# Two projection steps in token halves, with their weights loaded ahead of the third x tile, in a fused hybrid attention layer

## The reference

```
def rmsnorm(x, g):
    y = xf * lax.rsqrt(jnp.mean(xf * xf, axis=-1, keepdims=True) + RMS_EPS)
    return (y * g.astype(jnp.float32)).astype(x.dtype)
...
    h = rmsnorm(x, norm_g)
    proj = jnp.einsum('bsd,dc->bsc', h, w_in)
    a_qkv, z_a, b_qkv, z_b, r_a, r_b = jnp.split(proj, offs, axis=-1)
    # three dilated groups and MoBA on slices of proj, gated by silu(z)
    merged = sigmoid(r_a + b_merge[:D]) * y_a + sigmoid(r_b + b_merge[D:]) * y_b
    return x + jnp.einsum('bsd,de->bse', merged, w_out)   # then a last rmsnorm
```

## Time and profile before

| | us |
|---|---|
| median of 3 runs | 429.53 (429.46 to 429.69) |
| the profiled execution, its own time | 429.92 |
| its span, first to last instruction | 428.1 |
| PE busy | 417.7, 98% of the span |
| DVE, ACT, POOL busy | 302.8, 232.0, 220.9 |

### The profile page before, as it was taken

The page is one execution under the profiler, slowest core; times in us unless marked ns, Lnnn a source line. Parts: engine busy times, 40 slices in busy tenths (PEclk is TensorE's granted clock), DMA queues, the critical chain, the costliest instruction groups (busy, mean ns, idle before and its releaser), DMA issues.

```text
span 428.1 us, 7122 instructions
## 1 busy us (share of the span) xinstructions
PE 417.7 (98%) x2526; PEld 372.5 (87%) x2526; DVE 302.8 (71%) x520; ACT 232.0 (54%) x487; POOL 220.9 (52%) x158
## 2 busy tenths in 40 slices
PE   7899999999999999999999999999999999999994
PEld 6789998889889988998888888889999999988884
DVE  3879946385856777657865773696686768589956
ACT  5745557554864764657656563454454545532634
POOL 5954533252655634574459655444335433734790
PEclk9999999999999999999999999999999999999998
DMA  8893454937899768222421335540443134199905
GB/s 272 250 262 102 152 163 143 280 132 260 278 303 388 290 213 273 100 100 54 144 99 50 100 127 205 196 136 14 122 138 108 48 116 136 38 410 393 418 7 198
DMA packets 49187, 77.23 MB, mean 180 GB/s; under 512 B 4440, under 2 KB 39296, under 8 KB 47616
## 3 DMA queue, kind: packets, MB, share of 16 engines
q1 hardware_dynamic: 44256, 67.91, 47.9%
q10 hardware_dynamic: 4896, 8.86, 5.7%
HBM read 55.73 MB, written 14.74 MB: 165 GB/s over the span
## 4 chain that ended last, share of the span: by engine, by line
PE 94%; DMA 2%; ACT 1%; DVE 1%; issue 1%; SPq 0%; DVEq 0%; ACTq 0%
PE ps L1183 15%; PE ps L1187 15%; PE ps L1184 15%; PE ps L1408 5%; PE ps L1407 5%; PE ps L1406 5%; PE ps L1224 4%; PE ps L1226 4%; PE ps L1225 4%; PE ps L1296 4%; PE ps L1277 3%; PE ps L1455 3%; PE ps L1453 3%; PE ps L1454 3%; PE ps L1315 2%; PE ps L1337 2%
## 5 line engine op out<-in xcount | busy, mean ns | idle before, releaser
L993 POOL TENSOR_TENSOR w_lo<-raw,w_hi 128x1024 fp32r<-128x1024 f32 x39 | 96.8, 2483 | 103.5 <-ACT w_hi L1507 103.5
L1183 PE MATMUL ps<-hT_hi,w_hi 128*128 128x512 f32 x240 | 95.7, 399 | 1.1 <-DVE hT_lo L1913 1.1
L1187 PE MATMUL ps<-hT_lo,w_hi 128*128 128x512 f32 x240 | 93.8, 391 | 0.0
L1184 PE MATMUL ps<-hT_hi,w_lo 128*128 128x512 f32 x240 | 93.6, 390 | 0.0
L1075 POOL TENSOR_TENSOR w_lo<-raw,w_hi 128x512 fp32r<-128x512 f32 (+1 forms) x34 | 42.5, 1270 | 49.5 <-ACT w_hi L1529 49.5
L1187 PEld LDWEIGHTS ps<-hT_lo,w_hi 128*128 128x128 f32 x240 | 45.0, 188 | 9.9
L1183 PEld LDWEIGHTS ps<-hT_hi,w_hi 128*128 128x128 f32 x240 | 45.1, 188 | 8.4 <-issue 1.3
L1184 PEld LDWEIGHTS ps<-hT_hi,w_lo 128*128 128x128 f32 x240 | 45.2, 188 | 7.0
L1224 PE MATMUL ps<-w_hi,hT_hi 128*128 128x256 f32 x160 | 45.2, 283 | 0.0
L1226 PE MATMUL ps<-w_lo,hT_hi 128*128 128x256 f32 x160 | 44.7, 279 | 0.0
L1225 PE MATMUL ps<-w_hi,hT_lo 128*128 128x256 f32 x160 | 44.6, 279 | 0.0
(11 more groups left out here) (279 smaller groups left out, 1048.0 us busy)
## 6 DMA issues: line engine op xcount, KB each, us to landing
raw<-in_w_in SPq DMA_DIRECT2D x25, 1024.0 KB, 5.6
KTs<-KTs SPq DMA_DIRECT2D x20, 256.0 KB, 4.4
folds<-folded_early SPq DMA_DIRECT2D x4, 1024.0 KB, 9.3
wq_raw<-in_w_out SPq DMA_DIRECT2D x4, 1024.0 KB, 9.7
folded<-folds SPq DMA_DIRECT2D x4, 1024.0 KB, 6.4
t_three<-output_weight_sums SPq DMA_DIRECT2D x2, 2048.0 KB, 11.5
output_weight_sums<-ws_parts ACTq DMA_DIRECT2D x6, 512.0 KB, 6.1
raw<-in_w_out SPq DMA_DIRECT2D x3, 1024.0 KB, 5.0
```

The source lines that it names most:

```text
L993: nc.gpsimd.tensor_tensor(ring(w_lo, n, kt), src, ring(w_hi, n, kt).bitcast(F32), ALU.subtract).then_inc(lo_ready, 1)
L1183: pe.matmul(out, wh, hh, start=(k == 0), stop=False)
L1184: pe.matmul(out, wl, hh, start=False, stop=False)
L1187: return pe.matmul(out, wh, hl, start=False, stop=(k == kts - 1))
```

## The change

SP now issues x 0 and x 1, then the weights of steps 0 and 1 in two transfers of 512 KB, split by k (4 groups of 128 features each, 256 columns wide) and not by column, and then x 2 and x 3. Steps 0 and 1 are run together and in two halves of 256 tokens. The first half needs x 0 and x 1 only. PE turns these two, ACT and DVE split them by themselves (256 tokens a piece, 8 pieces), and PE runs the 48 products of 256 columns of the first half, both steps interleaved by k. Ahead of the last k it turns x 2 and x 3; then it finishes the first half and runs the 48 products of the second. The turned tiles no longer fit one bank each, because banks 0 and 1 hold the running results: a pair of tiles has six banks, two of them used twice, which adds waits of ACT and PE on hT_lo.

POOL splits the weights of steps 0 and 1 in four pieces of two k, each with both steps in it, high and low. The squares of x 1, x 2 and x 3 are now summed by ACT for the low half of the features and by DVE for the high half; DVE scales the low half and ACT the high half, except that DVE scales both halves of x 1. All these lie between the pieces of the first half on ACT and DVE.

```
-            for i in range(TT):
+            for i in range(2):
+                load_rows(i)
+            for e in range(2):
+                ks = slice(4 * e, 4 * e + 4)
+                sp.dma_start(first[:, ks, :], w_in_t[:, ks, at:at + 256]).then_inc(first_half_in[e], 16)
+            for i in range(2, TT):
+                load_rows(i)
...
+            for m in range(FIRST_PIECES - 1):
+                pool.wait_ge(first_half_in[m // 2], 16)
+                hi, lo, part = first_pieces(w_hi, m), first_pieces(w_lo, m), src[:, :, 2 * m:2 * m + 2, :]
+                nc.gpsimd.tensor_copy(hi, part).then_inc(first_hi, 1)
+                pool.wait_ge(first_hi, m + 1)
+                nc.gpsimd.tensor_tensor(lo, part, hi.bitcast(F32), ALU.subtract).then_inc(first_lo, 1)
...
+            for i in range(2):
+                turn_rows(i)
+            for k in range(KT_D):
+                if k == KT_D - 1:
+                    for i in range(2, TT):
+                        turn_rows(i)
+                for n in range(2):
+                    first_high(n, 0, k)
+                if k:
+                    first_lows(k - 1)
+            first_lows(KT_D - 1)
+            for n in range(2):
+                for k in range(KT_D):
+                    first_high(n, 1, k)
+                    first_low_weights(n, 1, k)
+                    if k:
+                        first_low_rows(n, 1, k - 1)
+                first_low_rows(n, 1, KT_D - 1)
...
+            square_rows(0, D)
+            root(0)
+            square_rows(1, D // 2)
+            scale_high_half(0)
+            root(1)
+            turned_high(0, range(4))
+            square_rows(2, D // 2)
+            turned_high(0, range(4, 6))
+            root(2)
+            square_rows(3, D // 2)
+            turned_high(0, range(6, KT_D))
+            scale_high_half(2)
+            root(3)
+            scale_high_half(3)
+            turned_high(1, range(KT_D))
...
+            variance(0)
+            square_high_half(1)
+            scale_rows(0, 0)
+            variance(1)
+            turn_vectors()
+            for half in range(2):
+                scale_rows(1, half)
+            turned_low(0, range(3))
+            square_high_half(2)
+            turned_low(0, range(3, 4))
+            variance(2)
+            turned_low(0, range(4, 6))
+            scale_rows(2, 0)
+            square_high_half(3)
+            turned_low(0, range(6, 7))
+            variance(3)
+            turned_low(0, range(7, KT_D))
+            scale_rows(3, 0)
+            turned_low(1, range(KT_D))
```

More of the change, by code:

```diff
@@ L1155, in _ @@
                 pe.matmul(ps[:, 0, 0:P], ident[:, :], ident[:, :], start=True, stop=True)
[L1157 to L1161, removed]
-                for k in range(KT_D):
[L1163 to L1172, removed]
+            pe.wait_ge(vec_in, 32)
@@ new lines, in first_high @@
+            def first_high(n, p, k):
+                if n == 0:
+                    pe.wait_ge(hT_hi_ready, KT_D * p + k + 1)
+                    if p == 0 and k < 6:
+                        pe.wait_ge(first_hi, k // 2 + 1)
+                    elif p == 0:
+                        pe.wait_ge(hi_ready, 2)
+                elif p == 0 and k == 0:
+                    pe.wait_ge(gb_ready, 1)
+                pe.matmul(ps[:, n, 256 * p:256 * p + 256], ring(w_hi, n, KT_D)[:, k, :], pair_of(hT_hi, p, k),
+                          start=(p == 0 and k == 0), stop=False)
@@ new lines, in first_low_weights, with first_low_rows @@
+            def first_low_weights(n, p, k):
+                if n == 0 and p == 0 and k < 6:
+                    pe.wait_ge(first_lo, k // 2 + 1)
+                elif n == 0 and p == 0:
+                    pe.wait_ge(lo_ready, 2)
+                pe.matmul(ps[:, n, 256 * p:256 * p + 256], ring(w_lo, n, KT_D)[:, k, :], pair_of(hT_hi, p, k),
+                          start=False, stop=False)
+            def first_low_rows(n, p, k):
+                if n == 0:
+                    pe.wait_ge(hT_lo_ready, KT_D * p + k + 1)
+                last = pe.matmul(ps[:, n, 256 * p:256 * p + 256], ring(w_hi, n, KT_D)[:, k, :],
+                                 pair_of(hT_lo, p, k), start=False, stop=(p == 1 and k == KT_D - 1))
+                if p == 1 and k == KT_D - 1:
+                    last.then_inc(projected, 1)
@@ L1340, in values @@
                 last.then_inc(valued, 1)
-            for s in range(NS):
+            for s in range(2, NS):
                 score, turn = [], []
@@ L1888, in turn_vectors @@
                 nc.vector.tensor_scalar(hbias[:], gb[:, 8:24], 0.5, None, ALU.mult).then_inc(gb_ready, 1)
-            for i in range(HALVED):
-                variance(i)
-                scale_rows(i, 0)
+            variance(0)
+            square_high_half(1)
+            scale_rows(0, 0)
+            variance(1)
             turn_vectors()
-            last, high = TT - 1, slice(D // 2, D)
-            variance(last - 1)
-            dve.wait_ge(x_in[last], 16)
-            link(nc.vector.scalar_tensor_tensor(out=squares[:, last, high], in0=xs[:, last, high], scalar=1.0,
-                                                in1=xs[:, last, high], op0=ALU.mult, op1=ALU.mult,
-                                                accum_out=ss_part[:, 0:1]))
```

171 lines of the change are left out of this document (87 added, 84 removed).

## The result

The changed kernel takes 431.10 us (median of 6 runs, 430.89 to 431.45), the kernel before beside it 429.72 (6 runs, 429.46 to 429.81). The ratio is 1.0030, 95% interval 1.0020 to 1.0041: slower by 0.3%, more than a measurement of this kernel blurs. The forecast was 429.7, in a range of 428.2 to 431.0. The profiled execution took 430.89 with a span of 429.1.

What follows compares the result with a forecast made beforehand. PE is busy 98%, its start held by x's loading, then by POOL's weight splits. Fourth cast at 15.4 to 16.0 plus 9.6 put step 2 at 25.4, 0.2 later: 429.53 + 0.2 = 429.7 us, range 428.2 to 431.0.

Steps and rivals of the forecast that it cites:

- Bank 0 has to be emptied ... done at 24.9 if d_hex is through: Before step 2: ACT and DVE empty bank 0 by 24.9, ahead of step 2's start at 25.4.
- rival C: Step 2 waits for its bank or weights as d_hex meets POOL's subtraction; bank free at 26.4, 430.7 us; chance 0.08.
- The scale: From profiled execution to median of runs: the median is 0.4 below the profiled 429.92, so 429.53 + 0.2 = 429.7.
- the sum of 25.4: Start of step 2, forecast at 25.4 within 25.0 to 25.6, 0.2 later than the 25.17 before.
- S, the first product: Start of PE's first product in step 0: 9.3 to 10.7, taken as 9.8, 4.4 us earlier than 14.20.
- The pace of a 256-column product: PE's products in steps 0 and 1: 0.117 each, 96 of them 11.2, 0.3 more than before.
- POOL's pushes: DVE's scalings and half squares push POOL's weight splits back 1.1 to 1.7; fourth cast ends at 15.4 to 16.0.
- The end of the fourth cast + 9.6: PE's remaining work behind POOL's fourth cast: step 2 starts 9.6 after it, at 24.0 without any disturbance.
- rival B: x 3 late: DVE's waits for POOL add up to 3.8 to tile 3's chain; step 2 at 26.5, 430.8 us; chance 0.16.
- Rival A: Pushes not paid: fourth cast ends by 14.6, step 2 starts at 24.0 to 24.3, 428.4 us; chance 0.22.
- Do half squares contend?: DVE's half squares beside POOL: both counted as disturbing; if not, 1.1 less and step 2 at 24.3.
- Step 2's weights: Before step 2: ACT casts them in 1.05 from about 21.2, POOL subtracts in 2.4, ready at 24.7.

Runs made afterwards that it cites:

- experiment 3: The changed kernel with only the variance of x 1 to 3 given one tensor operand, d_hex left in place: 430.85 us, ratio 1.0026 to the kernel before.
- experiment 1: The changed kernel with the three d_hex instructions moved ahead of the second half's low parts: 430.73 us, ratio 1.0023 to the kernel before.
- Experiment 8: The kernel before, unchanged, profiled three more times: 429.11, 429.88 and 430.40 us, with step 2 starting at 24.35, 25.06 and 25.62.
- experiment 4: The kernel of experiment 1 with squares of x 2 and x 3 wholly on ACT, their variance back to one operand: 429.10 us, ratio 0.9987 to before.
- 5: The kernel of experiment 4 with ACT scaling the high half of x 1 instead of DVE: 428.98 us, ratio 0.9982 to the kernel before.
- experiment 7: The kernel before with only the load order changed, weights of steps 0 and 1 ahead of x 2 and x 3: 435.84 us, ratio 1.0143.

## Why the prediction was wrong, point by point

The miss is 431.10 less 429.7, 1.4 us. About half of it arose at step 2's start, the rest in going from the profiled execution to the median.

**The step that failed: "Bank 0 has to be emptied ... done at 24.9 if d_hex is through".** d_hex was not through. The prediction had this as rival C, "d_hex meets POOL's subtraction as it did at 19.07", priced at 26.4 with a chance of 0.08, and set aside because "POOL starts that subtraction only about 22.3, when d_hex should be through". The prediction's own figures left little room for that: the last low part at 21.6 and 0.8 for d_hex put its third instruction near 22.1, 0.2 ahead of POOL. POOL started at 21.89, 0.4 earlier, and d_hex's third instruction was asked at 22.02: it came 0.13 too late and so waited for nearly all of the 2.4. Both times hang on one event, the end of ACT's last high part, forecast at 21.2 and measured at 20.88. Behind it POOL was to start 1.1 later and started 1.01 later; DVE's last low part was to end 0.4 later and ended 0.71 later (21.59), which is where the cover was lost. So the two move together, and the lag of 0.12 or 0.13 stands in all three profiled executions with this order (21.89 and 22.02, 21.99 and 22.12, and 21.85 and 21.97 in experiment 3). Such a cover has no middle: it holds or it costs what is left of the other engine's instruction. 0.08 was far too low. The place was told by the earlier trace rows and the price by the earlier trace rows. It cost 0.67 at step 2 (25.37 to 26.04), shown by experiment 1, where the wait is gone, and by experiment 3, where it stays at 26.00 though the turning waits for nothing. The sign that the prediction named for C, PE idle between step 1 and step 2, is the one that the profile shows.

**The scale.** The sum was made against 25.17 and then 0.4 was subtracted to come from the profiled 429.92 to the median 429.53, as if the same would hold for the changed kernel. Experiment 8 shows what that 0.39 was: a late execution of a kernel whose start varies. The changed kernel's profiled execution was the lowest of its six runs, 0.21 below its median. So the 1.4 is made of 0.64 for the late bank (26.04 against 25.4), 0.1 of difference in the law, 0.4 that was taken off wrongly, and 0.2 between 430.89 and 431.10. Against 24.9, the start that the median of before stands for (experiment 8), the same 25.4 would have meant 0.5 more, and not 0.2.

The terms of the sum of 25.4; without the wait for the bank step 2 would have started at 25.37:
- **S, the first product**, 9.8 forecast, 10.22 measured. DVE's two scalings of x 1 took 2.33 and not 0.86, locked behind POOL's first subtraction (8.15 to 9.47). The weights landed earlier than thought (5.4 behind the issue at 1.6, so 7.0), and POOL was at work from 7.46. In experiment 1, the same code up to there, the two scalings took 1.23 and the first product started at 9.34, and the fourth cast was no earlier for it: this term decided nothing.
- **The pace of a 256-column product** was 0.120 and not 0.117: 96 x 0.003 is 0.3. The 0.117 came from a later step of the kernel, where the operands have the opposite places.
- **POOL's pushes** are real: casts of 0.61 took 0.81, 1.07 and 0.82, each beside a DVE scaling or square, and experiment 4 brings them back to 0.61. But they were over-counted at 1.1 to 1.7. The fourth cast ended at 14.75, 1.0 behind an undisturbed 7.46 + 3 x 1.9 + 0.61 = 13.8, and ahead of the forecast 15.4 to 16.0, in which POOL started at 8.0. (The prediction speaks of five disturbing instructions; it lists and sums four.) PE waited 0.9 in all ahead of the turning (38 products of 0.120 from 10.22 to 15.68), and not the 2 to 3 that were to be seen.
- **"The end of the fourth cast + 9.6"** was right where nothing came between (9.64 in experiments 3 and 4, 9.63 in 5) and became 10.6 in the change. All of the difference lies in the turning: from its start to the product behind it 2.66 pass (15.68 to 18.34), and 1.66 in experiment 3. PE's weight loads waited there 0.83 for the hT_lo that stood behind the variance of x 3, and 0.20 for the scaling of x 3. The variance was priced "variance, reciprocal and the two gb instructions 0.7 together", and 0.35 with its reciprocal in tile 3's chain, at nothing beside POOL. It is rival B on a small scale: tile 3's chain was late by a lock. (The order puts 38 products ahead of this turning and 58 behind it, as the prediction has it; the 44 given with PE's list ahead of it is wrong.)
- So 25.4 came out right by errors of opposite sign: the cast 0.6 to 1.2 too late, what follows it 1.0 too short. That is luck. **Rival A**, no pushes, did not happen in the change; experiments 4 and 5, which take most of the cause away, start step 2 at 24.42 and 24.09 (the prediction had 24.0 to 24.3), but their medians are 429.10 and 428.98 and not 428.4: the scale again.
- **Do half squares contend?** The prediction left this open, with 24.3 if they did not. They do: the casts beside them grew, and with the squares on ACT they are back at 0.61. That is what the Trainium skill, "SBUF — State Buffer", section "Who interferes with whom", states for DVE instructions with two SBUF inputs, and the trace agrees; it holds for the 2.43 of d_hex's third instruction as well.
- **Step 2's weights**, 24.7 forecast, were ready at 24.30, and x 3 was scaled at 17.43 to 17.65, inside the forecast 17.2 to 17.8. PEclk stayed at its upper level in the changed kernel, as said; that idle times of 1.4 never cost clock can't be said, since one of four executions of the kernel before lost it behind just that (experiment 8).

## What to carry to other kernels

Where two engines lock each other out, price a cover as a coin with two sides: either the instruction comes ahead of the other engine's, or it waits for all that is left of it; put constant work where the other engine is idle, and keep two-tensor instructions, even those of one element, off the queue that someone waits behind. Profile the kernel before more than once before summing against a start that depends on loads: here it spread by 1.3 us, as much as the whole effect. Where both sides of a cover hang on one event, sum the two short chains behind it and compare them; how late the event itself comes then falls out. And sum the corners together: two covers that end at the same time hide each other's worth.

## What the hardware showed that was not expected

- DVE's sum of two one-element operands took 0.15 where no subtraction of POOL ran, 0.72 and 1.99 beside POOL's subtraction; the same sum with one of them as a scalar operand 0.20 beside the same subtraction.
- Short instructions of DVE with a single tensor operand wait for POOL's subtraction as well: an int32 one of 128x128 took 1.31 against 0.22, and in experiment 7 a float32 one of 128x16 took 1.03 against 0.17. The conversion at 19.07 had shown the first.
- The granted clock of PE can fall in one execution and not in the next of the same kernel, behind the same idle time of 1.40: sixteen transposes took 3.23 and 1.97. What PE did before was not quite the same: it was busy 3.7 of the 5 us from 5 to 10 where the clock fell, and 4.0 where it stayed.
